# Paired value products and a softmax by query tile, a forget block stream by stream, backward states decayed by ScalarE, and token rows loaded first

## The reference

```python
def gqa_attend(q, k, v):                      # second block, layer 0: 16 heads of 64, 4 key-value heads
    s = jnp.einsum('bkgqd,bksd->bkgqs', q, k) * (HEAD_DIM ** -0.5)
    p = jax.nn.softmax(s, axis=-1).astype(v.dtype)
    return jnp.einsum('bkgqs,bksd->bkgqd', p, v)
# tokens attend 512 keys (context and tokens), the context attends its own 256:
#   o_l = gqa_attend(q_l, k_all, v_all);  o_c = gqa_attend(queries(h_ctx), k_c, v_c)

def gates(z):                                 # second block, layer 1 (hgrn2_mixer): forget gates
    f = lb + (1.0 - lb) * jax.nn.sigmoid(z)   # z = modulate(rms_norm(h)) @ w_in[...], both streams
    return heads(jnp.log(f)), heads(1.0 - f)

def step(state, inp):                         # hgrn2_chunk_scan, 4 chunks of 64, forward and flipped
    ...
    new_state = jnp.exp(L_end[:, :, 0, :])[..., None] * state + jnp.einsum(
        'bhsk,bhsv->bhkv', kc * jnp.exp(L_end - L), vc)
    return new_state, o_inter + o_intra
```

## Time and profile before

| | before |
|---|---|
| median of 3 runs | 3367.22 us (3360.96 to 3367.56) |
| profiled execution | 3359.6 us |
| its span in the trace | 3357.8 us |
| mean granted clock of PE | 0.976 |
| busy: PE, PE weight loads | 3138.8 us (93%), 2413.6 us |
| busy: DVE, ACT, POOL | 1809.7 us (54%), 700.8 us (21%), 38.0 us (1%) |
| DMA | 430.74 MB, mean 128 GB/s |

### The profile page before, as it was taken

One profiled execution on the slowest core, in us unless ns is written; L12 is line 12 of the kernel. 1 busy time (PEld: TensorE's weight loads), 2 busy tenths in 40 slices (PEclk: granted clock), 3 DMA queues, 4 the chain that ended last, 5 costly groups with the idle time before them and its releaser, 6 DMA issues.

```text
span 3357.8 us, 50695 instructions
## 1 busy us (share of the span) xinstructions
PE 3138.8 (93%) x21630; PEld 2413.6 (72%) x21630; DVE 1809.7 (54%) x2753; ACT 700.8 (21%) x1318; POOL 38.0 (1%) x76
## 2 busy tenths in 40 slices
PE   8999988999989999989899998998999998998998
PEld 8987774549967997765558984554888883465797
DVE  5554545556645555455556555564343561287565
ACT  1112213202112102223211112351211002143110
POOL 1000000000001000000000000000000000000000
PEclk9999999999999999999999999999999999998999
DMA  8644402226555745312226642200232342231352
GB/s 271 226 168 143 163 27 76 76 96 221 196 194 178 253 166 187 127 64 76 76 76 221 211 150 91 76 1 26 76 101 76 138 163 82 87 114 57 126 176 101
DMA packets 279695, 430.74 MB, mean 128 GB/s; under 512 B 9880, under 2 KB 147456, under 8 KB 279472
## 3 DMA queue, kind: packets, MB, share of 16 engines
q1 hardware_dynamic: 273920, 411.52, 36.2%
q0 software_dynamic: 5088, 14.86, 1.3%
q10 hardware_dynamic: 464, 1.12, 0.1%
HBM read 426.43 MB, written 1.05 MB: 127 GB/s over the span
## 4 chain that ended last, share of the span: by engine, by line
PE 79%; DVE 13%; ACT 4%; issue 2%; DMA 1%; DVEq 0%; ACTq 0%; POOL 0%
PE bank L443 78%; PE bank L446 2%; DVE arena L739 1%; DVE arena L3659 1%; DVE arena L3257 1%; ACT xT L990 1%; ACT xT L2807 1%; DVE arena L3235 1%; DVE arena L1758 1%; DVE arena L3580 0%; ACT arena L3131 0%; ACT arena L3122 0%; DVE stats L913 0%; DMA ring<-in_ple_w_gate 0%; DMA arena<-in_ln_b 0%
## 5 line engine op out<-in xcount | busy, mean ns | idle before, releaser
L443 PE MATMUL bank<-arena 128*128 128x128 f32 (+7 forms) x7068 | 810.4, 286 | 51.2 <-DVEq L3663 7.7
L443 PE MATMUL bank<-xT,ring 128*128 128x128 f32 (+2 forms) x4576 | 805.4, 336 | 17.5 <-ACTq L2815 9.8
L443 PEld LDWEIGHTS bank<-arena 128*128 128x128 f32 (+3 forms) x7068 | 680.8, 165 | 177.5 <-issue 37.2
L443 PEld LDWEIGHTS bank<-xT,ring 128*128 128x128 f32 x4576 | 677.8, 194 | 139.0 <-issue 72.0
L443 PE MATMUL bank<-ring,xT 128*128 128x512 f32 (+2 forms) x1408 | 588.3, 569 | 16.7 <-ACT xT L2807 7.1
L443 PEld LDWEIGHTS bank<-ring,xT 128*128 128x128 f32 x1408 | 258.7, 192 | 285.8 <-issue 268.5
L443 PE MATMUL bank<-ring,arena 128*128 128x256 f32 (+1 forms) x1584 | 439.4, 429 | 19.4 <-DVE arena L836 6.5
L443 PEld LDWEIGHTS bank<-ring,arena 128*128 128x128 f32 x1584 | 299.4, 191 | 134.4 <-issue 85.5
L779 DVE TENSOR_TENSOR arena<-arena,bank 128x256 f32<-128x256 f32 (+1 forms) x198 | 92.2, 466 | 429.5 <-PE bank L443 289.1
L691 ACT COPY arena<-bank 128x256 f32<-128x256 f32 (+1 forms) x264 | 107.8, 408 | 779.9 <-PE bank L443 778.9
L739 DVE TENSOR_TENSOR arena<-ring,arena 128x1024 f32<-128x1024 f32 (+1 forms) x216 | 257.1, 1191 | 7.4
(11 more groups left out here) (388 smaller groups left out, 2140.0 us busy)
## 6 DMA issues: line engine op xcount, KB each, us to landing
ring<-in_ffn_w SPq DMA_DIRECT2D x88, 1024.0 KB, 7.9
ring<-in_w_in SPq DMA_DIRECT2D x32, 2048.0 KB, 7.7
ring<-in_ffn_w_in SPq DMA_DIRECT2D x44, 1024.0 KB, 6.5
arena<-in_ada_w SPq DMA_DIRECT2D x18, 2048.0 KB, 13.6
ring<-in_ffn_w SPq DMA_DIRECT2D x16, 2048.0 KB, 7.9
ring<-in_ffn_w_out SPq DMA_DIRECT2D x12, 2048.0 KB, 8.1
ring<-in_hgrn_w_in SPq DMA_DIRECT2D x12, 2048.0 KB, 7.8
ring<-in_ffn_w SPq DMA_DIRECT2D x8, 1536.0 KB, 6.6
```

The source lines that it names most:

```text
L443: return self.e.matmul(o, lhsT, rhs, start=start, stop=stop, skip_group_check=True)
```

## The change

*Attention.* `weigh_pair` takes two heads of one key-value group at a time: for each block of 128 keys it issues the product of the even head into the lower 64 partitions of a bank and the product of the odd head into the upper 64 partitions of the same bank. It stands in every second iteration. DVE copies the pair out in one operation over 128 partitions. The transposed probabilities have four buffers, in the space of `qk_tok`, which is no longer in use then. In the token half the maximum, its negation, the exponential, the reciprocal and the scaling each go by query tile, with the semaphores counted by tile.

*First forget block.* The transposes of stream 0 and their evictions move into the last down half of the FFN, ahead of its second group; the callbacks `in_down` are now given the number of the half. The block multiplies stream 0 alone (256 columns), then come the transposes of stream 1, then the block's products of stream 1. ACT evicts in that order.

*States.* ACT multiplies the eight backward states of a step by their decay (`back_decayed`), and DVE adds the updates to four heads at once, 128x512 out of a bank, after its eight fused operations for the forward scan, which stay. The sigmoid of the output gates, which stood ahead, now stands between ACT's first and second step.

*Start.* x is the first load on ACT's queue, PE turns x before the parameter rows, ACT copies x before it makes the silu, and DVE forms the sums of x before it combines the first weight block.

```diff
         def act_first_loads(act):
 
+            act.e.dma_start(xtok[:], a["x"][0].rearrange("(t p) d -> p t d", p=P)).then_inc(x_landed, 16)
             act.e.dma_start(rows[0:8, :], a["c_2"][0].rearrange("(r p) -> r p", p=P)).then_inc(c_landed, 16)
...
-        PT = t(2, 4, SEQ)
+        t(2, 4, SEQ)
+        PT = qk_tok[:].rearrange("p a n -> p (a n)")[:, 0:4 * 4 * SEQ].rearrange("p (u k t) -> p u k t", u=4, k=4)
...
-            def weigh(u):
+            def weigh_pair(u):
                 h, s = units[u]
-                pe.wait_ge(PT_ready, pe.due(PT_ready))
+                pe.wait_ge(PT_ready, pe.due(PT_ready, 2))
                 nk = 4 if s == 0 else 2
-                par = h % 2
                 pe.wait_ge(to_dve.freed, to_dve.next_free())
                 bank = to_dve.free_bank()
                 for k in range(nk):
                     tt = k if s == 0 else 2 + k
-                    mm = pe.mm(bank[64 * par:64 * par + 64, 0:SEQ], av_tok[:, tt, (h // 4) * 64:(h // 4 + 1) * 64],
-                               PT[:, u % 2, k], k == 0, k == nk - 1)
-                    if k == nk - 1:
-                        mm.then_inc(to_dve.filled, 1)
+                    for par in range(2):
+                        mm = pe.mm(bank[64 * par:64 * par + 64, 0:SEQ], av_tok[:, tt, (h // 4) * 64:(h // 4 + 1) * 64],
+                                   PT[:, (u + par) % 4, k], k == 0, k == nk - 1)
+                mm.then_inc(to_dve.filled, 1)
 
             for u in range(len(units) + 2):
                 if u < len(units):
                     scores(u)
                 if 1 <= u <= len(units):
                     turn_probs(u - 1)
-                if u >= 2:
-                    weigh(u - 2)
+                if u >= 3 and u % 2:
+                    weigh_pair(u - 3)
...
             def exps(u):
                 h, s = units[u]
-                act.wait_ge(max_ready, act.due(max_ready))
+                if s:
+                    act.wait_ge(max_ready, act.due(max_ready))
                 if s == 0:
                     for qt in range(2):
+                        act.wait_ge(max_ready, act.due(max_ready))
                         act.wait_ge(to_act.filled, to_act.next_filled())
                         bank = to_act.filled_bank()
                         ins = e.activation(Pb[:, u % 2, qt], bank[:], ACT.Exp, scale=0.125,
...
                         act.wait_ge(to_act.freed, act.sent(to_act.freed))
+                        act.sem_inc(probs_ready, act.up(probs_ready))
...
                         ins = v.tensor_reduce(am[:, o + qt:o + qt + 1], bank[:], AX.X, ALU.max)
                         ins.then_inc(dve_step, dve.up(dve_step))
                         dve.wait_ge(dve_step, dve.sent(dve_step))
+                        ins = v.tensor_scalar(am[:, o + 2 + qt:o + 3 + qt], am[:, o + qt:o + qt + 1], -0.125, None, ALU.mult)
+                        ins.then_inc(max_ready, dve.up(max_ready))
+                        dve.wait_ge(max_ready, dve.sent(max_ready))
...
             def scale(u):
                 h, s = units[u]
-                dve.wait_ge(probs_ready, dve.due(probs_ready))
                 o = 2 * (u % 2)
                 r = am[:, 12 + o:14 + o]
-                v.reciprocal(r, am[:, 8 + o:10 + o]).then_inc(dve_step, dve.up(dve_step))
-                dve.wait_ge(dve_step, dve.sent(dve_step))
...
-                ins = v.tensor_copy(oT[r_, h // 2, s * SEQ:(s + 1) * SEQ], bank[r_, 0:SEQ])
+                ins = v.tensor_copy(oT[:, h // 2, s * SEQ:(s + 1) * SEQ], bank[:, 0:SEQ])
...
-                if u >= 3:
-                    keep_o(u - 3)
+                if u >= 4 and u % 2 == 0:
+                    keep_o(u - 4)
...
+        def pe_first_stream(pe, half, j):
+            if (half, j) == (3, 1):
+                pe.wait_ge(down_read, 2 * passes_before(pe.ffns) - 1)
+                pe_norm_mod(pe, (0,), xn_wide)
+
+        def act_first_stream(act, half):
+            if half == 3:
+                act_norm_evict(act, 1, 0, (0,))
+
         def pe_hgrn(pe):
             pe.wait_ge(xT_ready, pe.due(xT_ready))
 
-            def forget(gate_rows=None):
+            def forget(first=None):
                 for b in range(2):
                     blk = pe.block()
-                    pe_T(pe, blk, to_act, 0, [P] * 4, 512)
+                    if b == 0 and first:
+                        first(blk)
+                    else:
+                        pe_T(pe, blk, to_act, 0, [P] * 4, 512)
                     pe.used()
-                    if b == 0 and gate_rows:
-                        gate_rows()
+                    if b == 0 and first:
+                        pe_gate_rows(pe, (0,), hdiag)
+
+            def stream_by_stream(blk):
+                pe_T(pe, blk, to_act, 0, [P] * 4)
+                pe_norm_mod(pe, (1,), xn_wide)
+                pe.wait_ge(xT_ready, pe.due(xT_ready))
+                pe_T(pe, blk, to_act, 0, [P] * 4, SEQ, xT[:, :, SEQ:512])
...
-            forget(lambda: pe_gate_rows(pe, (0,), hdiag))
+            forget(stream_by_stream)
...
-                for k in range(KT):
+                for k in range(0 if back else 4, KT):
...
+            for g in range(2):
+                evict(hz[0][:, 0, 2 * g:2 * g + 2], ACT.Sigmoid)
+            act_norm_evict(act, 1, 0, (1,))
+            for g in range(2):
+                evict(hz[0][:, 1, 2 * g:2 * g + 2], ACT.Sigmoid)
             forget(0)
...
-            e.activation(h_gates, h_gates, ACT.Sigmoid).then_inc(act_step, act.up(act_step))
-            act.wait_ge(act_step, act.sent(act_step))
-            act.sem_inc(hgrn_in_ready, act.up(hgrn_in_ready))
+            act.wait_ge(ends_ready, act.due(ends_ready))
+            for i in range(3):
+                if i:
+                    act.wait_ge(back_state_ready, act.due(back_state_ready))
+                for h in range(KT):
+                    ins = e.activation(hS[1][i + 1][:, h], hS[1][i][:, h], ACT.Identity, scale=hend[1][:, h, 3 - i:4 - i])
+                    ins.then_inc(back_decayed, act.up(back_decayed))
+                act.wait_ge(back_decayed, act.sent(back_decayed))
+                if i == 0:
+                    e.activation(h_gates, h_gates, ACT.Sigmoid).then_inc(act_step, act.up(act_step))
+                    act.wait_ge(act_step, act.sent(act_step))
+                    act.sem_inc(hgrn_in_ready, act.up(hgrn_in_ready))
             act_prepare_sqrt(act)
...
+            dve.sem_inc(ends_ready, dve.up(ends_ready))
...
+                dve.wait_ge(back_decayed, dve.due(back_decayed, KT))
+                for b in range(2):
+                    dve.wait_ge(to_dve.filled, to_dve.next_filled())
+                    bank = to_dve.filled_bank()
+                    s = hS[1][i + 1][:, 4 * b:4 * b + 4]
+                    step(v.tensor_tensor(s, s, bank[:].rearrange("p (h n) -> p h n", h=4), ALU.add), to_dve.freed)
+                if i < 2:
+                    dve.sem_inc(back_state_ready, dve.up(back_state_ready))
             dve.sem_inc(state_ready, dve.up(state_ready))
...
-            pe_ffn7(pe, gate_rows_at(lambda: pe_gate_rows(pe, (0, 1), diag, to_act)))
-            pe_norm_mod(pe, (0, 1), xn_wide)
+            pe_ffn7(pe, gate_rows_at(lambda: pe_gate_rows(pe, (0, 1), diag, to_act)),
+                    lambda half, j: pe_first_stream(pe, half, j))
             pe_hgrn(pe)
...
         def first_act(act):
-            act_turn_c(act)
             act_turn_x(act, X2)
             act.sem_inc(ffn_x_ready, act.up(ffn_x_ready))
+            act_turn_c(act)
```

58 lines of the change are left out of this document (31 added, 27 removed).

## The result

The changed kernel takes 3338.13 us (median of 6 runs, 3335.24 to 3343.52) where the kernel before takes 3360.99 beside it (6 runs, 3357.86 to 3367.56; the three runs shown above are among them). The ratio is 0.9927, with a 95% interval of 0.9916 to 0.9939: 22.9 us, or 0.7%. The profiled execution took 3343.52 us, the longest of the six, with a span of 3341.7.

The account below looks back on a forecast made before the run. The chain of waits was read as 79% PE, 13% DVE, 4% ACT. Savings of 12 + 8.9 + 3.5 + 0.4 = 24.8 us off the profiled 3359.6, plus 4 towards the median, gave 3339 us; range 3328 to 3352.

Parts of the forecast that it names:

- Attention: forecast 12: Token half of attention: pairs and softmax by tile save 0.79 us a head, 12 us over 15 periods; context half 0.
- The loop of 4.66 us: Attention's token half before: DVE, ACT and DVE wait on each other in turn, 4.66 us a head.
- PE's 4.6 us: Attention's token half before: PE's weighing, scores and transposes for one head, 4.6 us, so PE is nearly full.
- the long period: Token half, heads where a weighed pair follows: 4.0 us between maxima, against 3.73 for the other heads.
- No overlap as a bound: Attention's lower bound: without overlap of a pair's products, the mean is 4.74 us a head, 1 us lost.
- The rival's premise: Attention's weighing: output halves don't overlap at 256 columns, so attention loses 1 instead of gaining 12; 3352 us, chance 0.09.
- Forget block: forecast 8.9: FFN to first forget block: stream by stream, the block ends at 2805.7 instead of 2814.6, 8.9 us saved.
- The rival in which the gap moves: First forget block gains 5, with the clock low after stream 1's wait; late decays, states gain 1.2; 3345 us, chance 0.12.
- States: forecast 3.5: State recurrence: last addition at 3074.9 instead of 3078.4, 3.5 us saved, with DVE waiting 1.4 for ACT in step 1.
- Start: forecast 0.4: Kernel start: PE begins the FFN near 19.4 instead of 20.16, at the low clock, and gains 0.4 us.
- only change places: Kernel start: DVE's sums of x, moved before its weight differences, were given no gain or loss of their own.
- The low clock as the slower case: Attention: PE falls to 1.2 GHz, losing 44 us in the token half, about 16 in the context half; 3411 us, chance 0.03.

Follow-up runs that it names:

- The products in sequence: The kernel before with both attention edits, but each pair issues all even-head products first, then all odd-head ones; 0.9989 of before, 3.7 us less.
- the load alone: The kernel before with one statement moved, x as first load on ACT's queue, the order on PE, ACT and DVE kept; ratio 1.0001 to before.

## Why the prediction was right

The forecast was 3339 us, the median is 3338.13. The sum of the four parts was 24.8 us; the edited stretches show 24.8 (24.5 that stay), and the timed difference is 22.9. That the sums agree so closely is luck, since the parts differ. So is the last microsecond of the time: the 24.8 were taken off 3359.6 + 4 = 3363.6, which is 2.6 us above the 3360.99 measured, and the gain was 1.9 smaller. Part by part:

*Attention: forecast 12, stretch 10.1 (10.5 alone).* The mechanism was right point by point. The loop of 4.66 us and PE's 4.6 were two bounds of nearly one height; neither edit alone moved the steady period (4.63 and 4.66), both together did. The sum had PE's 512-column record at 0.46 us, from the block that runs in part at the low clock; at full clock it is 27.70/64 = 0.43, and what fills the 4.66 up are some 0.3 us where one kind of product follows another (4.66 less 8 x 0.22, 4 x 0.43 and 8 x 0.11). The token half, from its first maximum to the context half's first, went from 76.63 to 63.47 us: 13.2 saved, a little over the forecast, though the long period was 4.15 and not 4.0: the first four heads alone save 4.3, one of which took 6.34 before. What the sum left out came behind it: 0.7 us in the context half, where periods of 3.72 and 4.45 follow waits of 1.60 and 2.04 us, and 2.3 in the product behind attention, both at a lower clock (0.77 from 2236 to 2242, 0.92 behind attention).

*No overlap as a bound: forecast 1 us lost.* The products in sequence kept half of the overlap and still saved 3.7 us. The rival's premise, that the halves don't overlap at 256 columns, is refuted by the 1.95 us for sixteen records.

*Forget block: forecast 8.9, measured 8.4 at its end.* The wait was 3.83 (3.8), the slow stretch cost 2.8 (I added 2), and 1.5 us were given back further on, which the sum had at nothing; 7.1 are left in the trace of the block alone. The rival in which the gap moves priced this at 5. Alone the edit timed at 5.4, with an interval of 2.7 to 8.4: it holds the rival's price and the 7.1 and leaves out the 8.9, so as a gain of the whole kernel this term was too large.

*States: forecast 3.5, measured 3.3 and 3.4.* The term was right by two errors that cancel. The fused operations and scaled copies come every 0.38 and 0.31 us, ACT was quicker than the 0.37 that I took, and DVE waits for no decay; it waits 0.84 us in each of two steps for PE's updates, which my sum left out.

*Start: forecast 0.4 with bounds of -0.8 and 1.6, measured 1.6 and 2.4.* This is the step that failed. I had x's first tile turned at 12.5, taking off the microsecond of its issue and the wait for the rows; but x landed 6.2 us after its issue instead of 11.5, and the turns began at 9.63. So ACT's silu was through at 16.79, where I had 19.4, and the last thing PE waits for is the weight block (17.38). I also wrote that DVE's sums "only change places": with the load alone the second product waits 2.56 us for them, and the gain is gone. What is left of the 2.8 us by which the changed kernel starts its FFN earlier is 1.6, since the first product takes 1.2 longer at the lower clock; with the start alone it takes 5.58, and 2.4 are left. In timed runs the whole part is within its noise, so it did not show in the result.

*The low clock as the slower case* did not happen: the granted clock was 1.00 in the token half (2175 to 2225) and 0.96 in the context half (2227 to 2275), where PE is busy for 31.99 of 48 us. The sum had nothing for it all the same, and it took the 3.0 us above.

Open is why the clock's losses scatter between executions. The traces show that they do, in unchanged code, by up to 8.5 us; no run here tells why. Open is also how much of the 22.9 us each part carries: by the ratios alone they sum to 9.8 + 5.4 + 4.0 + 0.7 = 19.9, with intervals of 3 to 4 us on either side of each.

## What to carry to other kernels

Where a loop through other engines and PE's own work are within a few per cent of each other, price edits to them together: here one alone was worth nothing and the other 4.0 us of the 9.8, and a run of the first alone would have thrown it away. Look for the product that waits longest behind a stage's first one before pricing an earlier start. When a gain of some us is measured in a kernel of milliseconds, align the two traces instruction by instruction, since unchanged stretches may scatter by as much as the gain.

## What the runs showed that was not expected

- Neighbouring products of 64 output columns and all 128 rows run two at a time where their halves alternate (16 records of 256 columns in 1.95 us), and still partly where eight records of one half are followed by eight of the other (0.91 us more instead of 1.75).
- The transfer of x landed 6.2 us after its issue when it was first on its queue and 11.5 when third, behind two of 4 KB. The parameter rows behind it on that queue landed 7.3 and 7.9 us after their issue instead of 12.1 and 12.4.
- A wait of 3.8 us ahead of 64 records was followed by a lower clock, 16.7 us instead of 14.0; one of 2.1 us was not. Elsewhere a wait of 2.20 us was followed by it and one of 2.22 was not.
- PE's clock fell to 0.87 in a stretch in which it was busy all the time, with products of 8 columns in it (1373 to 1400); the same stretch of the kernel before ran at 1.00.
